# mLSTM gate maxima broadcast by one fp32r pass over high and low rows, split on VectorE beside the input projection

## What is computed

```python
b = jnp.cumsum(lf, axis=1)
a = b + m[:, None, :]
d = b[:, :, None, :] - b[:, None, :, :] + ig[:, None, :, :]
d = jnp.where(causal[None, :, :, None], d, -jnp.inf)
m_t = jnp.maximum(a, d.max(axis=2))
w = jnp.einsum('btnd,bsnd->btsn', q, k) * jnp.exp(d - m_t[:, :, None, :])
```

## Time and profile before

| | |
|---|---|
| median of 3 runs (lowest to highest) | 1797.27 us (1795.65 to 1798.45) |
| span of the profiled execution | 1793.0 us |
| PE busy, of the span | 1682.9 us, 94% |
| DVE, ACT, POOL busy | 914.8, 609.5, 193.3 us |
| mean granted TensorE clock | 0.961 of full speed |

### The profile page before, as it was taken

The page is one execution under the profiler, slowest core; times in us unless marked ns, Lnnn a source line. Parts: engine busy times, 40 slices in busy tenths (PEclk is TensorE's granted clock), DMA queues, the critical chain, the costliest instruction groups (busy, mean ns, idle before and its releaser), DMA issues.

```text
span 1793.0 us, 37060 instructions
## 1 busy us (share of the span) xinstructions
PE 1682.9 (94%) x14727; PEld 1518.7 (85%) x14727; DVE 914.8 (51%) x2371; ACT 609.5 (34%) x1162; POOL 193.3 (11%) x316
## 2 busy tenths in 40 slices
PE   5899999978989999999989999898698999999998
PEld 3899975546989999999979998655488999999997
DVE  2534445646365645546463452475545654645554
ACT  2322126535143324223143222564233422413314
POOL 1011003442010000000001101154111000000001
PEclk9899989988989999999989998999888999999999
DMA  8435278356442222212123453743484221222201
GB/s 295 125 103 181 72 273 277 119 191 148 93 142 93 95 95 95 94 48 95 51 76 95 143 154 142 262 118 121 116 149 141 95 95 48 96 93 95 95 24 55
DMA packets 153326, 219.41 MB, mean 122 GB/s; under 512 B 11450, under 2 KB 112122, under 8 KB 152716
## 3 DMA queue, kind: packets, MB, share of 16 engines
q1 hardware_dynamic: 146736, 197.25, 34.9%
q0 software_dynamic: 6432, 19.91, 4.1%
HBM read 208.77 MB, written 16.68 MB: 126 GB/s over the span
## 4 chain that ended last, share of the span: by engine, by line
PE 87%; DVE 4%; ACT 2%; issue 2%; DMA 2%; POOL 1%; POOLq 1%; DVEq 0%; SPq 0%; ACTq 0%
PE ps L1271 28%; PE ps L1344 15%; PE ps L823 13%; PE ps L1231 6%; PE ps L697 2%; PE ps L940 2%; PE ps L868 2%; PE ps L955 2%; PE ps L911 1%; PE ps L809 1%; PE ps L1251 1%; PE ps L883 1%; PE ps L818 1%; PE ps L817 1%; DMA work<-in_x_sample 1%
## 5 line engine op out<-in xcount | busy, mean ns | idle before, releaser
L1271 PE MATMUL ps<-work_r,big_r 128*128 128x272 f32 x1344 | 279.2, 289 | 1.4 <-ACT work L1708 0.4
L1271 PE MATMUL ps<-work_r,slab_r 128*128 128x272 f32 x1344 | 278.5, 288 | 0.0
L1271 PE MATMUL ps<-xnT_r,big_r 128*128 128x272 f32 x1344 | 276.4, 287 | 0.0
L1271 PEld LDWEIGHTS ps<-work_r,big_r 128*128 128x128 f32 x1344 | 210.1, 188 | 3.9 <-issue 3.9
L823 PE MATMUL ps<-slab_r,work_r 128*128 128x256 f32 (+1 forms) x976 | 213.3, 285 | 0.0
L1271 PEld LDWEIGHTS ps<-xnT_r,big_r 128*128 128x128 f32 x1344 | 211.7, 188 | 0.0
L1271 PEld LDWEIGHTS ps<-work_r,slab_r 128*128 128x128 f32 x1344 | 210.5, 188 | 0.0
L1822 DVE TENSOR_TENSOR slab_r<-slab,big_r 128x2048 fp32r<-128x2048 f32 (+1 forms) x84 | 170.2, 2036 | 52.0 <-ACT big_r L1692 44.1
L823 PEld LDWEIGHTS ps<-slab_r,work_r 128*128 128x128 f32 x976 | 163.3, 191 | 2.7 <-issue 2.5
L1711 ACT ACTIVATE big<-big,work 128x560 f32<-128x560 f32 x44 | 33.6, 765 | 372.4 <-DVE big L2447 372.4
L1344 PE MATMUL ps<-side_r,big_r 128*128 128x272 f32 x696 | 145.6, 291 | 0.9 <-DVE big_r L1822 0.9
(11 more groups left out here) (467 smaller groups left out, 3200.1 us busy)
## 6 DMA issues: line engine op xcount, KB each, us to landing
slab<-in_w_mod SPq DMA_DIRECT2D x23, 2048.0 KB, 9.6
slab<-in_w_up SPq DMA_DIRECT2D x44, 1024.0 KB, 7.6
slab<-in_w_in SPq DMA_DIRECT2D x20, 1024.0 KB, 5.5
slab<-in_w_down SPq DMA_DIRECT2D x20, 1024.0 KB, 6.0
slab<-in_cache_cmp_kv SPq DMA_DIRECT2D x128, 128.0 KB, 2.0
slab<-in_cache_sel_kv SPq DMA_DIRECT2D x96, 128.0 KB, 2.0
big<-in_cache_win_kv SPq DMA_DIRECT2D x16, 512.0 KB, 6.6
out<-in_cache_win_kv POOLq DMA_DIRECT2D x16, 508.0 KB, 8.3
```

The lines of the kernel that those rows point to most:

```text
L1271: ins = mm(ps[2 * half + b][:, 0:HALF], wt, fr(x[:, k, HALF * b:HALF * b + HALF]), start=k == 0 and n == 0, stop=k == KC - 1 and n == 2)
```

## The change

The broadcast of the gate maxima becomes one fp32r matmul over 36 partitions in place of a plain fp32 matmul over 4. The 36 partitions are 64 to 99 of `side`: the rounded high parts of the four rows stand in 64 to 67, the low parts in 96 to 99, zeros between; the one-hot matrix has -1 at both places. At the start of each layer VectorE zeroes the 36 x 512 region and copies the one-hot matrix beside it, both as fp32r. In `gate_max`, ahead of the drain that raises gt_max, it rounds `Grow` (into `zero4`, whose zeros are used up by then), drains, copies the rounded rows to partitions 64 to 67 and writes the difference to 96 to 99.

```diff
@@ shape_constants
     for h in range(MH):
         oh[h, h] = -1
+        oh[64 + h, h] = -1
+        oh[96 + h, h] = -1
@@ trunk_program
+        Gparts, spread_rows = side[64:100, 0:SEQ], side[64:100, SEQ:2 * SEQ]
@@ PE, each head
-                    mm(ps[0][:, :], view("onehot", "p (h n) -> p h n", h=MH)[0:MH, h, :], Grow, start=True, stop=True).then_inc(ml_g.sem, 1)
+                    mm(ps[0][:, :], fr(spread_rows[:, 128 * h:128 * h + 128]), fr(Gparts), start=True, stop=True).then_inc(ml_g.sem, 1)
@@ DVE, start of each layer
                 V.memset(zero4, 0.0)
+                ts_(fr(Gparts), K["onehot"][64:100, :], 0.0, None, ALU.mult)
+                cp(fr(spread_rows), K["onehot"][64:100, :])
                 drain()
@@ DVE, gate_max
                     ts_(dg, ident[0:MH, 0:MH], Grow[:, SEQ - 1:SEQ], None, ALU.mult)
+                    cp(fr(zero4), Grow)
+                    drain()
+                    cp(fr(Gparts[0:MH, :]), fr(zero4).bitcast(F))
+                    tt(fr(Gparts[32:32 + MH, :]), Grow, fr(zero4).bitcast(F), ALU.subtract)
                     dve.drain().then_inc(gt_max.sem, 1)
```

## The result

| | before | changed |
|---|---|---|
| median of 4 runs (lowest to highest) | 1797.35 us (1795.65 to 1798.45) | 1786.34 us (1783.25 to 1790.48) |
| ratio, 95% interval | | 0.9945 [0.9925, 0.9965] |
| span of the profiled execution | 1793.0 us | 1788.6 us |
| mean granted TensorE clock in it | 0.961 | 0.962 |

The kernel is faster by 11.0 us, 0.6%, where 3.0 us were forecast; by the interval of the ratio it is between 6 and 14 us. Three executions that took more than 2700 us, two of the kernel before and one of the changed, are left out of every number of this document. The profiled execution of the changed kernel is the slowest of its four, 1790.48 us, and its span lies 1.9 us under its time.

What follows compares the result with a forecast made beforehand. The prediction took PE, busy for 94% of the span, as the bound. Broadcasts save 6.0 us and stalls add 3.0, so -3.0 us on the median 1797.27 gives 1794.3 us, range 1791.2 to 1798.3.

Steps and rivals of the forecast that it cites:

- The broadcast (0.30 us): Each head's gate-maxima broadcast on PE: 0.30 us instead of 1.05, saving 0.75 us, times 8 makes 6.0 us.
- The stall (1.5 us per layer): At the gate columns PE waits for VectorE's split ahead of gt_max: 1.5 us per layer, +3.0 us in all.
- The start of the layer (nothing): Two added 36 x 512 VectorE instructions delay it by up to 1 us, covered by 3.8 us; costed at nothing.
- The rest of a head (follows, moves nothing): VectorE's and ScalarE's work after each broadcast starts earlier or is covered, so it takes back none of the saving.
- The sum (-3.0): Whole kernel: -6.0 us from broadcasts plus 3.0 us of stalls, ends at -4.4 and -1.3 us.
- The second rival: First head regains full clock sooner, saving 1.5 us more per layer: -4.5 to -6.0 us in all; chance 0.15.
- The first rival (0.20): The gate-column stall brings PE's clock down behind it, costing 1.5 us per affected layer; both layers give 1797.3; chance 0.20.
- The third: VectorE's three split instructions are as slow as the scan, 1198 ns; stall 3.5 us per layer, 1801.3 us; chance 0.10.
- fourth rival: The heads' broadcast gets no shorter, so only the stall is left: +3.0 us, 1800.3 us; chance 0.05.

Runs made afterwards that it cites:

- head 0 alone: Late kernel with the fp32r broadcast for head 0 only, plain fp32 matmul over four rows for heads 1 to 3; 1794.53 us, ratio 0.9993.
- heads 1 to 3 alone: Late kernel with the fp32r broadcast for heads 1 to 3 only, old broadcast for head 0; 1790.87 us, ratio 0.9973.
- late kernel: Changed kernel with VectorE's three split instructions moved behind the drain that raises gt_max; 1786.61 and 1785.57 us, ratios 0.9923 and 0.9944.
- early loads: Late kernel with SyncE's modulation-weight loads issued at mod_acc instead of mod_t; 1786.14 and 1783.69 us, ratios 0.9941 and 0.9926.
- split alone: Changed kernel with VectorE's split kept but unused, broadcast back to plain fp32 over four rows; 1805.80 us, ratio 1.0040.
- Four passes: Late kernel with the fp32r broadcast issued four times in a row into the same bank at each head; 1782.93 us, ratio 0.9943.
- plain fp32: Late kernel with the broadcast over the same 36 rows, at partitions 64 to 99, as plain fp32 operands; 1783.51 us, ratio 0.9940.

## Why the prediction was off

*The broadcast (0.30 us).* Right where it goes ahead of the scores: 0.33. Missed at the even heads, where it overlaps with the scores and the saving is 1.05 (head 2 by its window), not 0.75. Over eight heads 7.2 us (head 0 alone and heads 1 to 3 alone, at full clock), not 6.0.

*The stall (1.5 us per layer).* Right: 1.43 and 1.39. VectorE was done 1.53 us later (1.56 worked out); the copies took 0.41 and 0.42 where 0.48 was worked out, the difference 0.69, and the gaps between them made up for it. The Trainium skill ("VectorE: DVE Perf Modes", "What auto-detection actually checks") says that an operation with one source and both sides in SBUF can handle two elements a cycle. The estimate of 0.42 for a copy that the prediction drew from that page is the measured time, for an output in fp32r too. The late kernel, at full clock 4.0 ± 1.0 us under the changed one, shows that no later wait gives the stall back.

*The start of the layer (nothing).* Right. Timeline of VectorE, changed kernel, beside the earlier trace rows:

```profile
65.87 0.43 DVE L1883 TENSOR_SCALAR side_r<-shape_constants 36x512 fp32r<-36x512 f32 x1
66.22 0.42 DVE L1884 CAST side_r<-shape_constants 36x512 fp32r<-36x512 f32 x1
...
68.93 0.51 DVE L2007 COPY big<-ps 128x280 f32<-128x280 f32 x2
```

The copy starts 0.26 later than before, and PE's second slab at 73.12 for 73.01 waits for nobody: it needs the copy 3.7 us later.

*The rest of a head (follows, moves nothing).* Wrong at head 3: PE comes 0.96 and 0.7 us too early for a slab of weights that is loaded by the pace of the parts before it. The prediction looked at VectorE and ScalarE there, not at SP's queue. The kernel with early loads shows the wait's cause, and that it was worth 0.36 to 1.65 us per layer in the traces (head 3 of the changed and the late kernel, less 17.66).

*The sum (-3.0).* For the work at full clock it was right: -4.0 ± 0.6 by the table, -2.8 to -3.3 by the traces. In part that is luck: the broadcasts gave more than forecast (-7.2 for -6.0), and the wait at head 3, which had no term, took about as much back. **The step that failed is that the heads keep their clock**: "Saved: 1.05 - 0.30 = 0.75 us", times 8, counts each broadcast by its own length alone and puts the clock behind it at nothing. The second rival, given 0.15, is what happened: the first head gets its clock back sooner. Its price of 1.5 us per layer came out at 1.7 (3.4 us less at half clock) or 3.4, in its head; over all executions, with what is lost behind the stall and elsewhere, at 2.2 per layer. So 1796.2 - 4.0 - 4.3 = 1787.9. Of the 11.0 us of the result another 2.6 are the luck of four executions; over all executions the change is worth 8.4.

*Its reason* was that the narrow matmuls of line 855 come 0.75 us sooner. They came 1.05 sooner, in all 20 first heads that gained clock and in none of those that did not. With four rows at partition 64 they did not, and the clock did not come (17.1 and 13.7 us). So the runs speak for this reason as much as for the rows; they do not tell the two apart.

*The first rival (0.20)* happened as well, in some executions: 1.5 us in layer 0 of two traces, nothing in the four other places. The Trainium skill's section on the clock's oscillation ("TensorE: Matmul & The Clock Gate", "HAM oscillation — how this bites in real kernels") says that waits between bursts halve the clock; here the same idle time of 1.35 us did so in four of eight places (two of the six above, and both of the split alone). The prediction leaned on the gate sums for this rival, and they are another case: PE has no wait there (busy for 2.44 of the 2.44 us from 81.49), only narrow matmuls. *The third and fourth rival* are excluded by the rows of the result: the difference took 0.69 us, not the scan's 1.20, and the broadcast 0.33 or nothing.

**What stays open.** Why the kernels with 36 rows at 64 to 99 get more clock than those with four: it is shown that they do, not how. At the first head the candidates are the rows and the narrow matmuls that come 1.05 us sooner; no run has four rows with the shorter way, or 36 rows at 64 with the longer one. Behind it they are the rows and, at head 2, the overlap. The zeros between the rows were not varied, and why four rows at 64 do not overlap with the scores is not known. In the 11 traces with 36 rows at heads 1 to 3 none of 66 such heads has more than 0.1 us at half clock; in the five with four rows 6 of 30 have, all of them in two passages through a layer, of ten; that alone could be chance. The 36 rows at partitions 0 to 35 gained no clock (140.9 us), but there PE stands idle for 2 us ahead of the first head, so place and idle time are not told apart. Four passes and plain fp32 have less time at half clock than late (122.4 against 133.2 ± 2.3), which six executions each do not settle. Four passes or plain fp32 with early loads was not run.

## What to carry to other kernels

Split a measured gain into work and clock before explaining it: the span less half of the time at half clock added up over the two parts of this change (7.2 and 8.0, each to 0.9), the time at half clock did not add up at all. Read the same sum from the traces too: for one kernel here the two differ by 2.4 us or more. Where narrow matmuls stand near the start of a stage, what shortens the way to them can be worth as much in clock as in its own length: here 1.7 or 3.4 us in a head whose broadcast gave 1.05. And a step that gets shorter should be followed to every queue that paces it, the weight loads too.

## What the runs showed of the hardware

- A matmul on partitions 64 to 99 started together with the next one on 0 to 63 (starts 0.00 and 0.01 us apart, fp32r and plain fp32), one on 0 to 35 with one on 64 to 127; sharing partitions, the fp32r pass of 512 columns goes 0.33 ahead. With four rows in use at 64 there was no overlap (1.06).
- Plain fp32 and four fp32r passes of 512 columns take the same, 0.97 to 1.06 us start to start.
- The same program spreads over 14 us from execution to execution (before: 1790.4 to 1804.5 us) and more of it lies in the clock than in the rest (standard deviations of 2.7 and 2.0 us). Two traces 4.4 us apart say little on a change of 8 us; 76 and 18 executions gave it to 1.0.
